# Rows of the new x transposed without rstd in a decoder block, and rstd multiplied onto each up projection's sum

## The reference

```python
def rmsnorm(x, g):
    xf = x.astype(jnp.float32)
    y = xf * lax.rsqrt(jnp.mean(xf * xf, axis=-1, keepdims=True) + EPS)
    return (y * g.astype(jnp.float32)).astype(x.dtype)
...
        x = x + rmsnorm(merged @ w_o[l], g_post_mix[l])

        h2 = rmsnorm(x, g_pre_ffn[l])
        u = causal_dwconv(h2 @ w_up[l], conv_w[l], conv_b[l])
        u_gate, u_val = jnp.split(u, 2, axis=-1)
        f = (jax.nn.gelu(u_gate, approximate=True) * u_val) @ w_down[l]
        x = x + rmsnorm(f, g_post_ffn[l])
```

## Time and profile before

| | |
|---|---|
| median of 3 runs | 1728.15 us (1727.6 to 1729.83) |
| the profiled execution | 1727.3 us, its span 1725.1 us |
| busy, TensorE | 1701.1 us (99%) |
| busy, VectorE | 1096.6 us (64%) |
| busy, ScalarE | 818.3 us (47%) |
| busy, GpSimd | 48.9 us (3%) |
| granted TensorE clock, mean | 0.998 |

### The profile page before, as it was taken

How to read it: one execution, slowest core, us unless ns; L and a number is a source line. 1 busy time by engine, 2 the same in 40 slices (tenths; PEclk the granted TensorE clock), 3 DMA queues, 4 the chain that set the end, 5 groups by cost and what they waited for, 6 DMA issues and landing times.

```text
span 1725.1 us, 26360 instructions
## 1 busy us (share of the span) xinstructions
PE 1701.1 (99%) x9590; PEld 1493.8 (87%) x9590; DVE 1096.6 (64%) x1444; ACT 818.3 (47%) x1103; POOL 48.9 (3%) x51
## 2 busy tenths in 40 slices
PE   7999999999999999999999999999999999999997
PEld 6998999999888888888888888888888888888886
DVE  6645567666575554554565677676776676676777
ACT  7433345444434444444444565454454455454453
POOL 1000000000040000000000000000000000000000
PEclk9999999999999999999999999999999999999999
DMA  9756478444655666666557465656665665656654
GB/s 298 225 187 183 135 221 253 143 125 144 209 169 171 196 195 195 218 194 192 189 182 242 161 190 189 195 187 190 190 191 186 193 194 185 194 187 191 195 181 137
DMA packets 245992, 327.79 MB, mean 190 GB/s; under 512 B 12907, under 2 KB 167308, under 8 KB 245388
## 3 DMA queue, kind: packets, MB, share of 16 engines
q1 hardware_dynamic: 245900, 326.47, 61.0%
HBM read 321.71 MB, written 3.67 MB: 189 GB/s over the span
## 4 chain that ended last, share of the span: by engine, by line
PE 97%; DVE 1%; issue 1%; DMA 1%; ACT 0%; POOLq 0%; POOL 0%; DVEq 0%; SPq 0%; ACTq 0%
PE bank L1397 18%; PE bank L1387 15%; PE bank L1388 15%; PE bank L1389 15%; PE bank L1401 10%; PE bank L1361 5%; PE bank L1363 4%; PE bank L1362 4%; PE bank L1374 1%; PE bank L1376 1%; PE bank L1375 1%; PE bank L1642 0%; PE bank L1643 0%; PE bank L1680 0%; PE bank L1659 0%
## 5 line engine op out<-in xcount | busy, mean ns | idle before, releaser
L861 DVE TENSOR_TENSOR wlo<-wraw,whi 128x1024 fp32r<-128x1024 f32 x580 | 710.8, 1232 | 454.1 <-ACT whi L589 452.0
L589 ACT ACTIVATE whi<-wraw 128x1024 fp32r<-128x1024 f32 x580 | 612.6, 1059 | 689.7 <-PE bank L1389 386.5
L1397 PE MATMUL bank<-hx,whi 128*128 128x512 f32 x1376 | 344.5, 392 | 0.0
L1397 PEld LDWEIGHTS bank<-hx,whi 128*128 128x128 f32 x1376 | 248.0, 189 | 44.9
L1401 PEld LDWEIGHTS bank<-hx,wlo 128*128 128x128 f32 x1376 | 187.7, 190 | 13.4
L1401 PE MATMUL bank<-hx,wlo 128*128 128x256 f32 x1376 | 191.9, 282 | 0.0
L1387 PE MATMUL bank<-whi,hx 128*128 128x512 f32 x448 | 175.7, 392 | 0.0
L1389 PE MATMUL bank<-whi,hx 128*128 128x512 f32 x448 | 174.4, 389 | 0.0
L1388 PE MATMUL bank<-wlo,hx 128*128 128x512 f32 x448 | 174.3, 389 | 0.0
L1361 PE MATMUL bank<-hx,whi 128*128 128x256 f32 x512 | 147.8, 289 | 12.5 <-DVE wlo L861 12.5
L1387 PE MATMUL bank<-whi,r_hi 128*128 128x512 f32 x384 | 149.8, 390 | 0.0
(11 more groups left out here) (258 smaller groups left out, 2135.2 us busy)
## 6 DMA issues: line engine op xcount, KB each, us to landing
wraw<-in_w_in SPq DMA_DIRECT2D x200, 512.0 KB, 3.7
wraw<-in_w_up SPq DMA_DIRECT2D x176, 512.0 KB, 4.3
wraw<-in_w_down SPq DMA_DIRECT2D x88, 512.0 KB, 4.2
wraw<-in_w_mem_kv SPq DMA_DIRECT2D x32, 512.0 KB, 3.7
wraw<-in_w_o SPq DMA_DIRECT2D x32, 512.0 KB, 4.4
wraw<-in_w_br_mem SPq DMA_DIRECT2D x16, 512.0 KB, 4.3
wraw<-in_w_br_nsa SPq DMA_DIRECT2D x16, 512.0 KB, 4.5
wraw<-in_w_br_ret SPq DMA_DIRECT2D x16, 512.0 KB, 4.3
```

The costliest lines, as they stand in the source:

```text
L589: nc.scalar.activation(whi[:, c], wraw[:, c], ACT.Copy).then_inc(hi_done, 1)
L861: V.tensor_tensor(wlo[:, c], wraw[:, c], whi[:, c].bitcast(F32), ALU.subtract).then_inc(lo_done, 1)
L1397: T.matmul(ps[UP_PAIRS[j][t]][:, :], whi[:, c, k, t * P:(t + 1) * P], hx[:, :, k0 + k, :], start=first and k == 0, stop=False, skip_group_ ...
```

## The change

The tiles are transposed as soon as their part of the new x is there, against the identity, without rstd. ScalarE and VectorE round the tiles with the gain as before. rstd comes onto the sums of the up projection instead. For the first group, by token, ScalarE multiplies it in when it copies the sum (a scale for each partition). For the 43 groups by feature, rstd is wanted along the free dimension: TensorE multiplies a tile of ones with the two diagonals (`second_rstd_to_rows`), VectorE copies the result once, and multiplies it onto each sum before the convolution, after waiting for the addition ahead of it. The squares of the new x are taken later: for half 0 behind ScalarE's tiles of half 0, for half 1 behind those of half 1. Both second mean squares and both diagonals stand on VectorE behind its tiles of half 1. On ScalarE the first four pairs of half 0 come ahead of the last sum's squares. The transposes of the first up sum move one chunk back. GpSimd fills the ones.

```diff
@@ scalar
             group_squares(3, 0)
             ahead(WO_LAST, (2, 3))
+            half_hi(0, range(4))
+            act.wait_ge(pe_done, 4 * WO_LAST + 4)
+            group_squares(3, 1)
+            half_hi(0, range(4, 8))
             for h in range(3):
                 row_squares(0, h)
-            act.wait_ge(pe_done, 4 * WO_LAST + 4)
-            group_squares(3, 1)
-            half_hi(0, range(4))
-            row_squares(1, 0)
-            half_hi(0, (4, 5))
-            row_squares(1, 1)
-            row_squares(1, 2)
-            half_hi(0, (6, 7))
             half_hi(1, range(8))
+            for h in range(3):
+                row_squares(1, h)
...
-                        e = nc.scalar.activation(arena[:, A_UB:A_UB + 512], ps[UP_PAIRS[0][0]][:, :], ACT.Copy)
+                        for t in range(TT):
+                            act.wait_ge(s_rstd, 5 + t)
+                            e = nc.scalar.activation(arena[:, A_UB + S * t:A_UB + S * (t + 1)], ps[UP_PAIRS[0][0]][:, S * t:S * (t + 1)],
+                                                     ACT.Copy, scale=st[:, 10 + t:11 + t])
@@ vector
-            ahead(WO_LAST, (2,))
-            dve.wait_ge(s_ssq, 3)
-            half_square(0, 6, 3, 1)
-            dve.wait_ge(s_rstd, 4)
-            diagonal(0)
+            ahead(WO_LAST, (2, 3))
+            half_lo(0, range(3))
             dve.wait_ge(s_sq, 8)
             half_square(1, 0, 4, 0)
             with_gain(3, 1)
             ch.wait()
             dve.sem_inc(evac[1], 1)
-            half_lo(0, (0, 1))
-            dve.wait_ge(s_rstd, 5)
+            half_lo(0, (3,))
+            dve.wait_ge(s_rstd, 4)
             residual(1, 0)
-            half_lo(0, (2, 3))
-            ahead(WO_LAST, (3,))
+            half_lo(0, (4, 5))
             residual(1, 1)
             residual(1, 2)
-            half_lo(0, (4, 5))
-            dve.wait_ge(s_ssq, 6)
-            half_square(1, 6, 3, 1)
             half_lo(0, (6, 7))
-            dve.wait_ge(s_rstd, 6)
-            diagonal(1)
...
             half_lo(1, range(8))
+            for t in range(TT):
+                dve.wait_ge(s_ssq, 3 * t + 3)
+                half_square(t, 6, 3, 1)
+            for t in range(TT):
+                dve.wait_ge(s_rstd, 5 + t)
+                diagonal(t)
...
+                        if isinstance(s, int) and n == 1:
+                            dve.wait_ge(s_r2, 1)
+                            ch.add(V.tensor_copy(arena[:, A_R2:A_R2 + S], ps[2][:, 0:S]))
+                            ch.wait()
+                            dve.sem_inc(s_r2c, 1)
                         dve.wait_ge(s_ub, 4 * s + (n + 1))
                         for t in range(TT):
                             e = V.tensor_tensor(up_tile(A_U, j, t), ps[UP_PAIRS[j][t]][:, 0:S], up_tile(A_UB, j, t), ALU.add)
+                        ch.link(e)
+                        e = V.tensor_tensor(both_tiles(A_U, j), both_tiles(A_U, j),
+                                            arena[:, A_R2:A_R2 + S].unsqueeze(1).to_broadcast([P, 2, S]), ALU.mult)
@@ tensor
-                        pe.wait_ge(s_dg, t + 1)
                         pe.wait_ge(s_trl, KT + 8 * t)
+                    if p in (0, 4, 6):
+
+                        pe.wait_ge(s_x2, 3 * t + {0: 1, 4: 2, 6: 3}[p])
...
-                        e = T.matmul(half_tile(t, k), X[:, t, k * P:(k + 1) * P], work[:, W_DIAG + P * t:W_DIAG + P * (t + 1)],
-                                     start=k % 2 == 0, stop=k % 2 == 1, skip_group_check=True)
+                        e = T.transpose(half_tile(t, k), X[:, t, k * P:(k + 1) * P], eye[:, :])
...
+            def second_rstd_to_rows():
+
+                pe.wait_ge(s_one2, 1)
+                pe.wait_ge(s_dg, 2)
+                for t in range(TT):
+                    e = T.matmul(ps[2][:, P * t:P * (t + 1)], work[:, W_ONE2:W_ONE2 + P], work[:, W_DIAG + P * t:W_DIAG + P * (t + 1)],
+                                 start=True, stop=True)
+                e.then_inc(s_r2, 1)
...
-                    quad(chunk_u, q + n, n % 2, up_group(s) + n // 2, H, {0: up_rows_transposes} if s == 0 and n == 1 else {})
+                    quad(chunk_u, q + n, n % 2, up_group(s) + n // 2, H, {1: up_rows_transposes, 3: second_rstd_to_rows} if s == 0 and n == 1 else {})
```

More of the change, by code:

```diff
@@ L91 @@
 W_Y, W_PROD, W_TMP = 0, 1024, 0
-W_DIAG = 2048
+W_DIAG, W_ONE2 = 2048, 2304
+A_R2 = 10240
 X2_PARTS = [(0, 1024), (1024, 1536), (1536, 2048)]
@@ L220, in build @@
         s_woh, s_dg, s_ut = sem("output_first_half"), sem("rstd_diagonal"), sem("up_transposed")
+        s_one2, s_r2, s_r2c = sem("second_ones"), sem("second_rstd_rows"), sem("second_rstd_rows_copied")
         s_ub, s_u, s_tap = sem("up_small_part"), sem("up_sum"), sem("conv_done")
@@ L254, in rstd_rows, with both_tiles @@
             return work[:, (W_RX, W_RM)[n]:(W_RX, W_RM)[n] + S]
+        def both_tiles(at, j):
+            return arena[:, at + 512 * j:at + 512 * (j + 1)].rearrange("p (u s) -> p u s", u=2)
         def diag_x(t):
@@ L552, in half_rstd @@
                 nc.gpsimd.tensor_tensor(st[:, at + 4:at + 5], st[:, at + 2:at + 3], half, ALU.pow).then_inc(s_rstd, 1)
+            nc.gpsimd.memset(work[:, W_ONE2:W_ONE2 + P], 1.0).then_inc(s_one2, 1)
             half_rstd(2, 0)
-            half_rstd(3, 6)
-            half_rstd(4, 1)
+            half_rstd(3, 1)
+            half_rstd(4, 6)
             half_rstd(5, 7)
@@ L1310, in _ @@
             with dve.Fori(0, (STEPS - 1) // 2) as i:
-                ch.enter(i, 16)
+                ch.enter(i, 24)
                 for u in range(2):
@@ L1320, in _ @@
                             split_lo(2 * i + (u + 1), 1 - u)
-                ch.leave((STEPS - 1) // 2, 16)
+                ch.leave((STEPS - 1) // 2, 24)
             dve.wait_ge(s_gpost, 32)
@@ L1811, in _ @@
             up_quads(Q0["up0"], 0)
+            pe.wait_ge(s_r2c, 1)
             for s in range(STEPS - 1):
```

## The result

The changed kernel takes 1733.29 us (median of 10 runs, 1732.91 to 1737.0), the kernel before 1728.06 us (10 runs, 1727.08 to 1731.11). The ratio is 1.0031, 95% interval 1.0022 to 1.004: 5.2 us slower, where 1729.8 us was forecast with an upper end of 1732.5. The prediction was wrong.

A forecast was written before the change was run, and what follows sets the result against it. TensorE was taken to bound the kernel. The terms +1.15 (Part 4, net of Parts 2 and 3), +0.4 (Part 5) and 0 (Part 6), taken as +1.6 us on the median 1728.15, gave 1729.8 us, range 1727.0 to 1732.5.

The forecast's parts named there:

- What bounds the kernel: TensorE, busy 1701.1 of 1725.1 us; only 22.4 us between projections and VectorE's work in the 700 us behind can move.
- Part 1, the transposes: 32 tiles of the new x: one record instead of two, TensorE spared 3.6 us, most of it turning into waiting.
- Part 2, half 0: Tiles and first up chunks of token half 0: first matmul 1.0 us earlier, the half's end 0.7 us earlier.
- Part 3, half 1: Token half 1: 9.7 us in place of 10.50; first up group ends 1.5 us earlier, half 0's gain included.
- Part 4, what is moved behind it: Squares and statistics ahead of the next up weights: second up group waits 2.6 us, starts 1.15 us later than before.
- Part 5: rstd as rows, two real matmuls of 128 columns behind the second up group: 0.4 us on TensorE.
- Part 6, the multiply: VectorE multiplies 43 up sums, 0.69 us each: no cost; 1.1 us left at the first down sum's deadline.
- The rival on the clock: The new 2.6 us pause lowers TensorE's pace behind it, 1.2 us lost, 1731.0 us; chance 0.09.

The follow-up runs named there:

- e6: The changed kernel with its 32 tiles transposed by real fp32 matmuls against the identity, two records each: 1733.87 us, ratio 1.0036.
- e1: The changed kernel with GpSimd's fill of the result rows waiting for the second up sum: 1731.62 us, ratio 1.0012.
- e2: The changed kernel with both diagonals made by an instruction on two SBUF tensors, the fill left in place: 1731.64 us, ratio 1.0015.
- e3: The changed kernel with 19 unused matmuls in TensorE's wait ahead of the second up group: 1732.99 us, ratio 1.0019.
- e10: e1 with 10 unused matmuls in TensorE's wait ahead of the second up group: 1730.19 us, ratio 1.0007 to the kernel before.

## Why the prediction was wrong, step by step

- **What bounds the kernel**: right. All that the change moved lies in the 30 to 40 us between the projections. From 1045 to 1708 TensorE is busy all the time in the changed kernel too.
- **Part 1, the transposes**: right. One record instead of two, 0.1 us a tile, and most of the saving turns into waits (e6: 1.1 us of 3.6 us are left at the second up group).
- **Part 2, half 0**: forecast 11.25 us from the first transpose to half 1's, measured 11.15 us (976.45 to 987.60). The single waits were smaller than forecast: 0.60, 0 and 0.69 us for 0.85, 0.4 and 0.85.
- **Part 3, half 1**: first matmul 2.26 us behind its transposes (forecast 2.27). The first group ends 1.7 us earlier than before, forecast 1.5.
- **Part 4, what is moved behind it**: this step failed, and on one point. The squares took 2.4 us and the statistics came as the rows said; e1, which has no collision, starts the second group 23.2 us behind the first transpose, against 23.6 in my working, and waits 2.5 us where I had 2.6. What the step left out is GpSimd's fill. I followed ScalarE's and VectorE's queues past the moved statistics, but not GpSimd's, where the fill stands behind the rstd of half 1 and now starts as soon as this is done. The fill then met the second diagonal: 3.50 us for 0.28, 2.1 us of it on the path.
- **Part 5**: 0.36 us for 0.4. Right.
- **Part 6, the multiply**: 43 of them at the size expected, and the tight place has 0.95 us left (forecast 1.1): the first down sum is added at 1358.93, and TensorE takes the bank at 1359.88. The changed kernel's group of multiplies, and its timeline at that place:

```profile
L1281 DVE TENSOR_TENSOR arena<-arena 128x512 f32<-128x512 f32 x43 | 29.8, 692 | 1.5
...
1357.65 1.28 DVE L1318 TENSOR_TENSOR arena<-bank,arena 128x512 f32<-128x512 f32 x2
...
1359.88 0.39 PE L1400 MATMUL bank<-whi,r_hi 128*128 128x512 f32 x1
```

- **The rival on the clock** had 0.09 and 1.2 us. It is what happened, and mis-sized: 2.2 us behind the 4.6 us wait, 1.3 to 1.6 us behind the 2.5 us one (e2, e1). Its evidence against, that a pause of 1.33 us left the pace alone, says nothing of one twice as long. I also took the 12.5 us of the earlier trace rows as all at the start; 2.00 us of them are the pause at 38.69, closer in length to my 2.6 us, and the pace behind it was full in that trace. That one trace would have misled me, since the same pause was followed by the slow pace in eight others. With a wait of 2.6 us and the pace of e1 my sum would have been 1.55 + 1.6 = 3.2 us, 1731.3 us. The collision adds 2.1 us of wait and 0.6 us of pace, and the other parts came out 0.4 us below my working: 5.45 us.

The term that was missing in the sum of part 4 is thus 2.1 us for the collision, and the term put at nothing is 2.2 us for the pace. Both omissions have one root: the new wait was priced by its length alone, and neither what may lengthen it nor what it does to the engine that waits was followed.

## What to carry to other kernels

Before moving an instruction, follow every queue on which something moves, the one of the least busy engine too, and ask what each released instruction will run beside in its new place. A wait of TensorE costs its length and, from some 2 us on in these runs, often a slow pace behind it; work that nobody needs soon belongs behind the weights of the next group, not ahead of them. A transpose, or any other saving on the engine that waits for others, is worth only what the chain of the others lets through.

## What the runs showed of the hardware

A fill by GpSimd (3.5 us) held a VectorE product of one SBUF tensor with a scalar for its whole length (3.50 us for 0.28) and a product of two SBUF tensors not at all (0.29 us). Instructions that VectorE started behind the held one kept their usual spacing and ended only with it (3.30 us for 1.22). After a pause of TensorE of 1.3 us its pace was full in every trace. After one of 2.0 us it was full in five traces, and in eight the granted clock was halved for a while, at 1.3 to 1.5 us lost. After 2.5 us a chunk of 2.87 us took 4.21 and 4.44 us, after 4.6 us 4.42 to 5.08 us, with a granted clock of 0.54 in the changed kernel; matmuls without use in the pause kept it full (e3, e10). So one trace doesn't tell what a pause costs. And before the change has its first effect, two executions of the same work were 3.3 us apart (0.2 us by the first matmul, 1.5 by the slow start, 1.5 by the pause at 39 us): more than half of the effect that was to be measured, so the stretch inside the trace decided more than the whole times.
